# Two modulation chunks of layer 0 move from the attention's matmuls to VectorE sums beside the branch units

## The reference, cut to what matters

```
mod   = silu(c)     @ w_mod[l] + b_mod[l]        # w_mod[l]: 1024 x 6144
mod_c = silu(c_ctx) @ w_mod[l] + b_mod[l]
sh1, sc1, g1, sh2, sc2, g2 = split(mod, 6)       # the same for mod_c
h1   = modulate(rms_norm(h, norm1_g), sh1, sc1)
p, u, v, q, k, val, gates = split(h1 @ w_in[l])  # 2304 + 3 x 1024 columns
pool_o, sgu_o, attn_o = pool_mix(p), sgu_mix(u, v), neighbourhood_attention(q, k, val, ...)
y    = sig(gp) * (pool_o @ w_po) + sig(gs) * (sgu_o @ w_so) + sig(ga) * (attn_o @ w_ao)
h    = h + g1 * (y @ w_o)
h    = h + g2 * (square(relu(modulate(rms_norm(h, norm2_g), sh2, sc2) @ w_ff1)) @ w_ff2)
```

## Time and profile before

| | us |
|---|---|
| median of 3 runs (2003.71 to 2009.75) | 2003.89 |
| the profiled execution | 2004.48 |
| its span in the trace | 2002.6 |
| PE busy in the span | 1940.7 (97%) |
| DVE, ACT, POOL busy | 1261.5, 885.9, 167.0 |
| PE share of the chain that ended last | 86% |
| neighbourhood attention of layer 0, from the second pair's scores to the first branch unit | 57.4 |
| neighbourhood attention of layer 1, the same stretch, two thirds of the pairs | 30.7 |

### The profile page before, as it was taken

The page is one execution under the profiler, slowest core; times in us unless marked ns, Lnnn a source line. Parts: engine busy times, 40 slices in busy tenths (PEclk is TensorE's granted clock), DMA queues, the critical chain, the costliest instruction groups (busy, mean ns, idle before and its releaser), DMA issues.

```text
span 2002.6 us, 33109 instructions
## 1 busy us (share of the span) xinstructions
PE 1940.7 (97%) x13572; PEld 1703.3 (85%) x13572; DVE 1261.5 (63%) x2184; ACT 885.9 (44%) x1508; POOL 167.0 (8%) x187
## 2 busy tenths in 40 slices
PE   7999999999999999999999999999999999999998
PEld 7769999998689999978688887888888998997887
DVE  6765666677556666544434447667677745677776
ACT  5655543445565444424532334322232536455443
POOL 0220000002103100002511000000000012000000
PEclk9999999999999999999999999999999999999999
DMA  7365699955646565323533333454656422664554
GB/s 239 102 214 165 157 234 220 220 171 165 224 145 189 182 214 161 116 77 125 163 96 100 95 106 110 133 179 155 197 180 198 139 85 62 186 195 140 182 183 137
DMA packets 313325, 317.56 MB, mean 159 GB/s; under 512 B 17079, under 2 KB 291398, under 8 KB 312918
## 3 DMA queue, kind: packets, MB, share of 16 engines
q1 hardware_dynamic: 308156, 301.65, 49.6%
q0 software_dynamic: 3904, 12.03, 3.0%
q10 hardware_dynamic: 1114, 1.76, 0.3%
HBM read 306.54 MB, written 8.85 MB: 157 GB/s over the span
## 4 chain that ended last, share of the span: by engine, by line
PE 86%; DVE 7%; ACT 3%; DMA 2%; issue 1%; POOL 0%; SPq 0%; DVEq 0%; ACTq 0%; POOLq 0%
PE acc L696 20%; PE acc L697 19%; PE acc L698 19%; PE acc L746 8%; PE acc L745 4%; DVE w_low L2024 3%; PE pss L921 2%; PE acc L742 1%; PE acc L711 1%; ACT w_high L1473 1%; PE pst L933 1%; PE acc L712 1%; PE acc L713 1%; DMA raw<-in_w_mod 1%; PE acc L948 1%
## 5 line engine op out<-in xcount | busy, mean ns | idle before, releaser
L2024 DVE TENSOR_TENSOR w_low<-raw,w_high 128x1024 fp32r<-128x1024 f32 (+4 forms) x503 | 561.1, 1156 | 140.5 <-ACT w_high L1473 137.3
L1473 ACT ACTIVATE w_high<-raw 128x1024 fp32r<-128x1024 f32 (+4 forms) x503 | 471.7, 984 | 375.6 <-PE acc L698 234.2
L696 PE MATMUL acc<-normed,w_high 128*128 128x256 f32 (+1 forms) x1768 | 565.6, 320 | 0.7 <-DVE w_low L2024 0.6
L698 PE MATMUL acc<-normed,w_low 128*128 128x256 f32 (+1 forms) x1768 | 560.6, 317 | 0.0
L697 PE MATMUL acc<-normed,w_high 128*128 128x256 f32 (+1 forms) x1768 | 560.6, 317 | 0.0
L696 PEld LDWEIGHTS acc<-normed,w_high 128*128 128x128 f32 x1768 | 336.1, 190 | 27.0 <-issue 2.0
L698 PEld LDWEIGHTS acc<-normed,w_low 128*128 128x128 f32 x1768 | 336.2, 190 | 22.5
L697 PEld LDWEIGHTS acc<-normed,w_high 128*128 128x128 f32 x1768 | 336.3, 190 | 22.0
L746 PE MATMUL acc<-inner,w_high 128*128 128x512 f32 x612 | 218.2, 396 | 0.0
L696 PE MATMUL acc<-inner,w_high 128*128 128x512 f32 (+2 forms) x576 | 197.3, 343 | 2.2 <-DVE w_low L2024 2.0
L697 PE MATMUL acc<-inner,w_high 128*128 128x512 f32 (+2 forms) x576 | 196.0, 340 | 0.0
(11 more groups left out here) (281 smaller groups left out, 2685.9 us busy)
## 6 DMA issues: line engine op xcount, KB each, us to landing
raw<-in_w_ff SPq DMA_DIRECT2D x128, 512.0 KB, 4.2
raw<-in_w_mod SPq DMA_DIRECT2D x96, 512.0 KB, 4.4
raw<-in_w_in SPq DMA_DIRECT2D x84, 512.0 KB, 4.1
raw<-in_l_w_gate SPq DMA_DIRECT2D x44, 512.0 KB, 5.5
raw<-in_l_w_up SPq DMA_DIRECT2D x44, 512.0 KB, 4.5
raw<-in_l_w_down SPq DMA_DIRECT2D x32, 512.0 KB, 4.5
raw<-in_l_w_qkv SPq DMA_DIRECT2D x24, 512.0 KB, 4.6
raw<-in_l_w_out SPq DMA_DIRECT2D x16, 512.0 KB, 4.4
```

The source lines that it names most:

```text
L696: mm(dst, lh, rh, start=i == 0, stop=False)
L698: ins = mm(dst, ll, rh, start=False, stop=i == n - 1)
L1473: nc.scalar.activation(WH[:, s % NSPLIT, w0:w0 + nw], RAW[:, r:r + nw], ACT.Copy).then_inc(w_high, 1)
L2024: V.tensor_tensor(WL[:, s % NSPLIT, c], RAW[:, r:r + nw], WH[:, s % NSPLIT, c].bitcast(F32), ALU.subtract).then_inc(w_low, 1)
```

## The change

The last two chunks of layer 0 leave way (1) for way (2). `mod_units` ends at 4 x 1024, `modulation(MODS)` before the branch units is gone, and the neighbourhood attention of layer 0 runs with `mods` = 0. Behind each of the branch units t = 4 to 19 stands one late unit of 128 rows by 1024 columns: eight for chunk 4, eight for chunk 5, two vectors each. On DVE two `late_op` follow the `w_low` of unit t+2. PE sums the rows after units 13 and 21 and turns them after units 14 and 22; `mod_gain(0, 1)` moves behind the 24 units.

```diff
-            return 2 if q < 2 else 1
+            return 2 if q < 4 else 1
 
         def mod_sum(q, s):
-            return wk(D * q, D) if s else (view(ROPE, 0, (D,)) if q % 2 == 0 else wk(2 * D, D))
+            if q == 0:
+                return wk((4 + s) * D, D)
+            if q == 1:
+                return view(MASK, 0, (D,)) if s else view(ROPE, 0, (D,))
+            return wk(D * (q - 2), D) if s else (view(ROPE, 0, (D,)) if q % 2 == 0 else wk(2 * D, D))
...
-        mod_units = [(0, c) for c in range(0, 6 * D, 256)]
+        mod_units = [(0, c) for c in range(0, 4 * D, 256)]
...
-        late_mods = []
+        late_mods, EARLY = [], 16
+
+        def beside(l, t):
+
+            return l == 0 and 4 <= t < 4 + EARLY
 
         def late_modulation():
 
-            q, j = (len(late_mods) // 8, len(late_mods) % 8) if len(late_mods) < 16 else \
-                (2 + (len(late_mods) - 16) // 4, 2 * ((len(late_mods) - 16) % 4))
-            n = 1 if q < 2 else 2
-            unit(part(kp(A["w_mod_2"][1])[:, j:j + n, D * q:D * q + D], 0, D), words=n * D, split=False)
+            at = len(late_mods)
+            if at < EARLY + 16:
+                q, j, n = at // 8, at % 8, 1
+            else:
+                q, j, n = 4 + (at - EARLY - 16) // 4, 2 * ((at - EARLY - 16) % 4), 2
+            l, c = (0, q + 4) if q < 2 else (1, q - 2)
+            unit(part(kp(A["w_mod_2"][l])[:, j:j + n, D * c:D * c + D], 0, D), words=n * D, split=False)
...
-            if l == 0:
-                modulation(MODS)
             for b, (name, kt) in enumerate(BR):
                 for m in range(0, D, P):
                     unit(part(w[:, :, 2304 + b * D + m:2304 + b * D + m + P], 0, P),
                          part(kp(A[name][l])[:, :, m:m + P], 8 * P, P), words=(8 + kt) * P)
+                    if beside(l, KD * b + m // P):
+                        late_modulation()
...
+        early_rows = (13, 21)
...
-                attention(na_tasks(l), 0 if l else MODS, lead=lambda: values(1, blocks=[0, 1, 2, 3]), tail=gate_tail,
+                attention(na_tasks(l), lead=lambda: values(1, blocks=[0, 1, 2, 3]), tail=gate_tail,
...
                         used()
+                        t = KD * b + m
+                        if beside(l, t):
+                            assert not order[st["unit"]][0]
+                            st["unit"] += 1
+                        if l == 0 and t in early_rows:
+                            late_rows(early_rows.index(t))
+                        if l == 0 and t - 1 in early_rows:
+                            late_columns(early_rows.index(t - 1))
...
                 for b3 in range(3):
                     for m in range(KD):
+                        if l == 0 and KD * b3 + m - 1 in early_rows:
+                            late_copy(early_rows.index(KD * b3 + m - 1))
...
-                attention(na_tasks(l), 0 if l else MODS)
-                mod_gain(l, 1)
+                attention(na_tasks(l))
+                if l:
+                    mod_gain(l, 1)
...
                         split()
+                        if beside(l, KD * b3 + m):
+                            late_op()
+                            late_op()
+                if l == 0:
+                    late_known(2)
+                    mod_gain(l, 1)
```

More of the change, by code:

```diff
@@ L411, in build @@
                             late_modulation()
-        assert len(mod_used) == len(mod_units) and late_mods[-1] == (5, 6, 2)
+        assert len(mod_used) == len(mod_units) and late_mods[-1] == (7, 6, 2)
         split_ids = [i for i, u in enumerate(order) if u[0]]
@@ L587, in build @@
         raw_free = {}
-        mod_ready = [16, 32, 40, 48, 56, 64]
-        mod_end = [sum(q <= p for q, j, n in late_mods) for p in range(6)]
+        mod_ready = [16, 32, 48, 64, 72, 80, 88, 96]
+        mod_end = [sum(q <= p for q, j, n in late_mods) for p in range(8)]
         pair_bank, cols_bank = {}, {}
@@ L655, in _ @@
             st = {"phase": 0, "acc": 0, "unit": 0, "split": 0, "task": 0, "sq": 0, "freed": 0, "store": 0,
-                  "pair": 0, "rope": 0, "spread": 0, "steps": 0}
+                  "pair": 0, "rope": 0, "spread": 0, "steps": EARLY}
             mm = nc.tensor.matmul
@@ L856, in late_step @@
             def late_step(step):
-                if step - 3 in mod_end:
+                if step - 3 in mod_end[2:]:
                     late_columns(mod_end.index(step - 3))
-                if step - 2 in mod_end:
+                if step - 2 in mod_end[2:]:
                     late_rows(mod_end.index(step - 2))
@@ L1059, in last_product @@
                 turned(wb, four[0:2], far, 4, S)
-                late_rows(5)
+                late_rows(7)
                 turned(wb, four[2:4], far, 4, S)
@@ L1239, in _ @@
                     values(1, blocks=blocks, ready=one_by_one())
-                    late_columns(5)
+                    late_columns(7)
                     values(1, blocks=blocks)
@@ L1307, in _ @@
                 pe.wait_ge(cols_free, st["pair"])
-                for src, kt in ((pot(T), 2), (sot(T), 2), (ot_na(T), 4)):
+                for b, (src, kt) in enumerate(((pot(T), 2), (sot(T), 2), (ot_na(T), 4))):
                     for m in range(KD):
@@ L1449, in _ @@
             st = {"phase": 0, "chain": 0, "acc": 0, "task": 0, "sig": 0, "split": 0, "store": 0, "res": [], "lot": 0,
-                  "pair": 0, "roots": 0, "steps": 0}
+                  "pair": 0, "roots": 0, "steps": EARLY}
             go = lambda: fence(act, st)
@@ L1658, in late_step @@
                 st["steps"] += 1
-                if st["steps"] - 3 in mod_end:
+                if st["steps"] - 3 in mod_end[2:]:
                     late_copy(mod_end.index(st["steps"] - 3))
@@ L1899, in _ @@
                 na_lead(0)
-                attention(na_tasks(l), 0 if l else MODS, lead=lambda: na_lead(1))
+                attention(na_tasks(l), lead=lambda: na_lead(1))
                 for b3 in range(3):
                     for m in range(KD):
+                        if l == 0 and KD * b3 + m - 1 in early_rows:
+                            late_copy(early_rows.index(KD * b3 + m - 1))
                         b, free = bank()
@@ L1981, in _ @@
                             half_squares(1, g + 2, 2)
-                            late_copy(5)
+                            late_copy(7)
                             half_squares(1, g + 3, 4)
@@ L2225, in late_op @@
                     if q > 1:
-                        dve.wait_ge(mod_summed, q - 1)
+                        dve.wait_ge(mod_summed, max(q - 1, 2))
                     ins = V.tensor_scalar(acc, w, part, None, ALU.mult)
@@ L2240, in late_known @@
                     dve.wait_ge(late_turned, q + 1)
-                    m, bm = 48 + KD * q, vcol["b_mod_2"] + 48 + KD * q
+                    m, bm = 32 + KD * q, vcol["b_mod_2"] + 32 + KD * q
                     for s in range(vectors(q)):
@@ L2590, in _ @@
                     split(2)
-                    late_known(6)
+                    late_known(8)
                     g = st["acc"] + 1
@@ L2728, in _ @@
                                 late_op()
-                            late_known(4)
+                            late_known(6)
                             residual_half(0, 48 * l + 40, 1)
@@ L2739, in _ @@
                             residual_half(4, 48 * l + 40, 1)
-                            late_known(5)
+                            late_known(7)
                             residual_half(6, 48 * l + 40, 1)
```

## The result

| | before | changed |
|---|---|---|
| median of the runs, us | 2005.11 | 2027.59 |
| ratio, with its 95% interval | | 1.011 (1.0095 to 1.0125) |
| the profiled execution, us | 2004.48 | 2023.82 |
| its span, us | 2002.6 | 2021.9 |

The kernel got slower by 22 us, 1.1%. The forecast was 2020 with a range of 2008 to 2034: the sign and the mechanism came as forecast, the size came 6 to 7 us above it. The changed kernel's profiled execution was the fastest of its four; it reached the attention's second pair 3.1 us earlier than the one of before (926.98 against 930.09 us), in work that the change doesn't touch. So the traces are compared from that point on.

A forecast was written before the change was run, and what follows sets the result against it. PE was taken as the bound, busy 1940.7 of 2002.6 us. Attention -11.4, ring loop +25.6 and row sums +1.5 gave +15.7 on the profiled 2004.48: 2020 us, range 2008 to 2034.

The forecast's parts named there:

- The attention gets shorter: Layer 0's neighbourhood attention, priced by layer 1's timeline, takes 45.0 us against 56.4 before: -11.4 us.
- none of these engines ended the waits: In layer 0's attention, ACT, DVE and SP, which lose work by the change, ended none of the waits.
- DVE's time is not the problem: Branch units: DVE's own work plus 2.48 us of `late_op` stays below PE's 6.80 us narrow, 8.16 wide.
- The ring's loop: Branch units: landing, split, two `late_op` and load issue make rounds of 9.26 us narrow, 9.52 wide: +25.6 us.
- The first and second row sums: PE's sums over partitions and turns: first pair falls into idle time, second pair is open, +1.5 us.
- `late_known` and `mod_gain` at nothing: Behind unit 23, a few small DVE instructions while PE works through the first unit of w_o: no cost.
- Starts 9.3 apart: Sign in the branch units: starts of `w_high` lie 9.3 us apart.
- PE idle 26 us: Sign in branch units: PE idle 2.5 us in each of units 9 to 16, less in 17 to 21, some 26.
- The loads come in time: Rival: the ring's wait in the branch units is always met early, total -8.3, 1996 us; chance 6%.
- Quick loads: Rival: landings near 3.2 us in the branch units, loop costs 12.1, sum +2.2, 2006.7 us; chance 6%.
- Crowded loads: Rival: late load and branch part share the engines with the gate part, 4.8 us per landing, 2031 us; chance 10%.
- The clock: Rival: PE's clock falls from 2.4 to 1.2 GHz in half of 14 stalled branch units, 2050 us; chance 3%.

The follow-up runs named there:

- e4: The kernel before with modulation chunks 4 and 5 of layer 0 left out altogether and a second transposing bank in the attention: ratio 0.994 to the kernel before.
- e2: The changed kernel with both `late_op` on DVE ahead of the split of unit t+2 instead of behind it: ratio 0.9963 to the kernel before.
- e1: The changed kernel with POOL's sixteen additions to the bias table waiting for the second `late_op`: ratio 1.0089 to the kernel before.
- e3: The changed kernel with SP issuing each late unit's load one place later, behind that of split unit t+2: ratio 0.9966 to the kernel before.
- e7: The changed kernel with the alterations of e2 and e3 together: ratio 0.9982 to the kernel before.
- e6: The changed kernel measured again, unaltered: ratio 1.0111 to the kernel before.

## Why the prediction was right, and where its sum was off

1. **The attention gets shorter: right, 0.9 us too much.** Taken was 11.4, measured 10.5 (the changed kernel and e4 agree). The pairs up to the last scores took 959.10 - 926.98 = 32.1 us for 31.8, the end of the attention 13.8 for 13.2. The plain subtraction, 10.1 us of removed matmuls, was nearer than the reading of layer 1's timeline: PE's busy time in the stretch fell by 10.43 (53.75 to 43.32), its idle time only from 3.66 to 3.56. The prediction's "none of these engines ended the waits" was a misreading: of PE's waits there, 3.5 us in all, DVE ended 1.9 and ACT 1.6. After the change 3.4 us of waits are left, ended by POOL and DVE, so the misreading cost nothing.
2. **DVE's time is not the problem: right** (e2: DVE 65% busy, no stall).
3. **The ring's loop: right in place, order and size, but one term was too small.** Predicted were 25.6 us, measured 30.95. Taken term by term for a narrow round: landing 4.1 (3.97 in the round shown, median 4.0), split 2.65 (2.57 to the start of the first `late_op`), issue 0.03 (0.07), two `late_op` 2.48 (2.95). The mis-sized term is "then two `late_op`, 2.48", the price from the earlier trace rows: it comes from the MLP, where POOL does nothing, while beside the branch units POOL adds up the bias table of layer 1. The prediction counted what DVE, ACT, SP and PE do there and left out POOL, though its 5.1 us busy stood in the earlier trace rows. With POOL away (e1) the loop costs 26.8, and the eight narrow rounds fit to 0.1 us. The 1.2 us left are in the six wide rounds, 58.2 us in e1 for 57.1: from issue to `w_high` four of their loads took 4.2 us and one 4.6, the `late_op` of one round stood 0.27 us later behind the two additions of `late_known`, and in the split of unit 16 `w_low` began some 0.4 us later than in the others, for which no run gives a cause.
4. **The first and second row sums: right in size, 1.5 against 1.7 us** for the open one (1.27 behind unit 21 and 0.46 behind 22); the first fell into idle time, as said, and costs 1.73 as soon as PE does not idle (e2, e3).
5. **`late_known` and `mod_gain` at nothing: right.** The stretch from the split behind unit 22 to the next is 0.46 us longer, the same in e2 and e3 and absent in e4. That is PE's turn of chunk 5 (0.53 by the earlier trace rows): the turn of chunk 4, with no `mod_gain` near it, also costs 0.46 in e3.
6. **The sum.** -10.5 + 30.95 + 1.7 = +22.1, and the medians say +22.5. The forecast's +15.7 lacks 0.9 of the attention, 4.2 of POOL, 1.2 of the wide rounds and 0.2 of the sums. No row of before had POOL's addition and a `late_op` side by side, so that its price could only be bounded, and it was not.
7. **The signs that were named.** `w_high` waiting for a DMA, loads issued right behind a `late_op`, no stall in the last two units: all there. (The trace puts one of these waits, that of unit 16, down to PE, but its `w_high` began 4.2 us after the issue of its load, like the others.) Starts 9.3 apart: 9.5. PE idle 26 us: only 19.8 in 13 waits for `w_low`. The rest of the 30.95 is 1.7 of row sum and turn, 0.8 of waiting for ACT's copy of the rows, some 5 of slow clock (below) and, by an estimate, some 3.5 at the waits' edges: before one wait the last matmul starts at 1030.46, then come 1033.38 and 1033.71, which with 0.23 from start to start in the run is 0.26 more than the 2.53 that count as idle. That sign was too simple: what the loop adds is the round, and PE may fill it with idle time or with slow work.

**The rivals.** "The loads come in time" needed landings under 1.6 us; they took 4. "Quick loads" of 3.2 us did not occur in the loop. "Crowded loads" of 4.8: the gate load is issued first and landed in 4.0, the late load behind it had the 4.8; its landing is not in the loop. "The clock" came true in small: see below.

## What to carry to other kernels

A buffer that is shared in the order of loading makes dependences between things that have nothing to do with each other: before work is added beside a stage, write down for each load whose words it takes over and which instruction frees them, and add up the round. Here it was longer than the unit by 2.8 us (9.56 against 6.80), with no engine full; one line moved on DVE or one on SP turned +1.1% into -0.35%. Such repairs don't add up (e7), so each is tried alone. And a duration is taken from a place where the same neighbours work, POOL included.

## What the runs showed of the hardware that was not expected

**DVE and POOL block each other.** POOL's addition of 128x256, reading two tables in SBUF, takes 0.73 us alone. Issued 0.16 us into the first of two `late_op`, it took 1.71: it ended 0.7 us after the start of the second. And the second `late_op`, which started meanwhile, took 1.76 for 1.28. One round of the changed kernel instruction by instruction, and the round in which chunk 5 begins:

```profile
1090.07 1.28 DVE L2253 SCALAR_TENSOR_TENSOR rope<-raw,silc,rope 128x1024 f32<-128x1024 f32 x1
1090.23 1.71 POOL L1449 TENSOR_TENSOR bias<-bias,cst 128x256 f32<-128x256 f32 x1 [7.58 <-DVE w_low L2047]
1091.27 1.76 DVE L2253 SCALAR_TENSOR_TENSOR mask<-raw,silc,mask 128x1024 f32<-128x1024 f32 x1
...
1081.47 1.18 POOL L1449 TENSOR_TENSOR bias<-bias,cst 128x256 f32<-128x256 f32 x1 [7.98 <-DVE w_low L2047]
1081.97 1.23 DVE L2250 TENSOR_SCALAR mask<-raw,silc 128x1024 f32<-128x1024 f32 x1
```

The last row is the first `late_op` of a chunk, which reads one tensor and one value per partition; it was held up too, 1.23 us for 0.75, and POOL's addition took 1.18. What the first three rows show vanishes when POOL is moved by one wait (e1). The Trainium skill, SBUF — State Buffer, section Who interferes with whom, states this rule: a VectorE instruction with two inputs in SBUF contends with a GpSimd instruction that reads SBUF. It calls the shared ports an exclusive lock and says that the order of issue decides who blocks. `late_op` reads `raw` and its accumulator, so it is such an instruction; the trace agrees on both sides, with 1.0 us for the one and 0.48 for the other.

**TensorE's clock fell in the stalling loop, three times, and cost nothing that can be seen.** Stretches of 10 us of the changed kernel (columns as in the earlier trace rows):

```profile
1030.00:1040.00 10.00, 7.47 (x26) 5.73 (x25) 5.71 (x6) 1.84 (x3) 1.71 (x1) 0.83 0.43 135
1070.00:1080.00 10.00, 8.24 (x30) 6.63 (x30) 5.89 (x7) 2.17 (x6) 1.71 (x1) 0.83 0.37 119
1100.00:1110.00 10.00, 9.29 (x34) 7.50 (x35) 5.99 (x8) 2.06 (x3) 1.71 (x1) 0.83 0.41 131
```

A granted clock of 0.83 over 10 us is 3.4 us at the lower level of 1.2 GHz and the rest at 2.4, so some 1.7 us of PE's time each, 5 in all. It went into what would have been idle time: the first two rounds with a fall are as long as the ones before them (9.56 from 1030.67 to 1040.23 after 9.64, 9.68 from 1068.99 to 1078.67 after 9.75), and in the third PE began unit 17 at 1110.71, when its `w_low` had just ended (1108.83 + 1.83), so the load held it and not the clock. The stretches between had 1.00 with as little work. In e6, the same kernel, the clock fell once (0.83 from 1030 to 1040 us) and the units took 0.8 us less, while the thirteen loads of the units 8 to 20 took 1.0 us less in sum from issue to `w_high`, so no price of the clock shows. In e2, where PE doesn't idle, the clock stayed at 1.00 from 1000 to 1150 us. The rival with the clock had the right event, but in three of fourteen rounds it stayed below what the loop left free.
